# A four-stage hybrid trunk on one core: gate and up weights handed over separately, the down product's PSUM banks one by one, and an 80-row meta matrix

## What is computed

```python
for i in range(DEPTH):                      # DEPTH = 2
    mix = pool_mixer(...) if i == 0 else latent_attention_mixer(...)
    x = layer_norm(ALPHA * x + mix, ...)
    x = layer_norm(ALPHA * x + swiglu(x, w_gate[i], w_up[i], w_down[i]), ...)

def swiglu(h, w_gate, w_up, w_down):        # 1024 x 2816, 1024 x 2816, 2816 x 1024
    return (silu(h @ w_gate) * (h @ w_up)) @ w_down
```

## Time and profile before

| | us |
|---|---|
| median of 3 runs | 2686.84 |
| lowest and highest | 2685.57 and 2687.7 |
| the profiled execution's own time | 2684.7 |
| its span, first to last instruction | 2682.9 |

### The profile page before, as it was taken

How to read it: one execution, slowest core, us unless ns; L and a number is a source line. 1 busy time by engine, 2 the same in 40 slices (tenths; PEclk the granted TensorE clock), 3 DMA queues, 4 the chain that set the end, 5 groups by cost and what they waited for, 6 DMA issues and landing times.

```text
span 2682.9 us, 34788 instructions
## 1 busy us (share of the span) xinstructions
PE 2553.1 (95%) x13203; PEld 2122.1 (79%) x13203; DVE 1005.3 (37%) x1489; ACT 567.6 (21%) x948; POOL 585.6 (22%) x290
## 2 busy tenths in 40 slices
PE   8899999999999889899999999988999999999996
PEld 7789888898889776585857584447889988899885
DVE  3433333333333642333333333422333333333336
ACT  2411011110111342332323232433111111111112
POOL 2422222222222410000000000232222222222225
PEclk9999999999999989999999999988999999999998
DMA  5201110111101111000000002232101111011111
GB/s 165 55 24 47 47 47 23 47 47 47 47 23 47 44 48 43 16 1 31 0 19 12 16 0 75 80 122 55 46 25 47 47 47 40 30 47 47 47 31 67
DMA packets 130114, 117.37 MB, mean 44 GB/s; under 512 B 8704, under 2 KB 117208, under 8 KB 130048
## 3 DMA queue, kind: packets, MB, share of 16 engines
q1 hardware_dynamic: 130064, 116.70, 14.6%
HBM read 110.81 MB, written 6.42 MB: 44 GB/s over the span
## 4 chain that ended last, share of the span: by engine, by line
PE 92%; DVE 4%; issue 2%; ACT 1%; POOL 0%; DMA 0%; SPq 0%; ACTq 0%; DVEq 0%
PE ps L557 22%; PE ps L558 21%; PE ps L559 21%; PE ps L922 4%; PE ps L911 4%; PE ps L806 2%; PE ps L895 2%; PE ps L978 1%; PE ps L780 1%; PE ps L822 1%; PE ps L811 1%; PE ps L627 1%; PE ps L953 1%; PE ps L851 1%; PE ps L937 1%
## 5 line engine op out<-in xcount | busy, mean ns | idle before, releaser
L557 PE MATMUL ps<-XH,WGH 128*128 128x368 f32 x2112 | 699.8, 331 | 17.6 <-POOL WGL L1700 13.5
L558 PE MATMUL ps<-XL,WGH 128*128 128x368 f32 x2112 | 700.0, 331 | 0.0
L559 PE MATMUL ps<-XH,WGL 128*128 128x368 f32 x2112 | 697.2, 330 | 0.0
L1452 DVE TENSOR_TENSOR XR<-XR,ps 128x1024 f32<-128x1024 f32 x378 | 461.5, 1221 | 105.7 <-PE ps L559 105.7
L557 PEld LDWEIGHTS ps<-XH,WGH 128*128 128x128 f32 x2112 | 398.5, 189 | 22.3 <-issue 18.9
L1437 DVE TENSOR_TENSOR HF<-SG,ps 128x368 f32<-128x368 f32 x132 | 71.0, 538 | 917.8 <-PE ps L559 912.6
L558 PEld LDWEIGHTS ps<-XL,WGH 128*128 128x128 f32 x2112 | 398.0, 188 | 1.8
L559 PEld LDWEIGHTS ps<-XH,WGL 128*128 128x128 f32 x2112 | 398.2, 189 | 0.0
L557 PE MATMUL ps<-WDH,HH 128*128 128x512 f32 (+1 forms) x792 | 329.4, 416 | 9.6 <-DVE XR L1452 9.6
L1691 POOL TENSOR_TENSOR HL<-HF,HH 128x368 fp32r<-128x368 f32 x132 | 129.8, 983 | 853.0 <-DVE HH L1441 853.0
L559 PE MATMUL ps<-WDH,HL 128*128 128x512 f32 (+1 forms) x792 | 314.9, 398 | 0.0
(11 more groups left out here) (205 smaller groups left out, 2725.8 us busy)
## 6 DMA issues: line engine op xcount, KB each, us to landing
RAWG<-ffn_w_gate SPq DMA_DIRECT2D x44, 512.0 KB, 4.7
RAWG<-ffn_w_up SPq DMA_DIRECT2D x44, 512.0 KB, 5.9
RAWD<-ffn_w_down SPq DMA_DIRECT2D x44, 512.0 KB, 3.7
CR<-cache_mla_l SPq DMA_DIRECT2D x64, 160.0 KB, 2.6
XR<-x_prompt SPq DMA_DIRECT2D x8, 512.0 KB, 12.4
WOP<-mla_w_o SPq DMA_DIRECT2D x4, 1024.0 KB, 5.0
WOA<-mla_w_o SPq DMA_DIRECT2D x1, 4096.0 KB, 17.3
o_y_prompt<-XR SPq DMA_DIRECT2D x8, 512.0 KB, 2.6
```

The lines of the kernel that those rows point to most:

```text
L557: pe.matmul(out, w[0], x[0], start=start, stop=False)
L558: pe.matmul(out, w[0], x[1], start=False, stop=False)
L559: return pe.matmul(out, w[1], x[0], start=False, stop=stop)
L1452: dve.tensor_tensor(XR[0:r, t, :], XR[0:r, t, :], bank2(4 + 2 * w, r), ALU.add).then_inc(s_row[2 * l + 1], 1)
```

## The change

- **Gate and up weights.** Loads, splits and handovers are made for each of the two apart. SP counts them in `f_raw[l][0]` and `f_raw[l][1]`; ACT copies 1024 elements twice, the gate half as soon as the last gate product of the block before is done (`f_gmm`), the up half after the last up product (`f_umm`). POOL subtracts twice. TensorE waits for the gate half ahead of the first gate product, and for the up half ahead of the first up product. ACT's copy of the gate half stands ahead of the third silu of a block, and POOL's two subtractions stand ahead of its third `HL`. SP loads block 1 of gate and up ahead of the next layer norm's gain and bias, and down of block 1 behind them.
- **Down product.** Waits and counts go by single banks: three matmuls, one addition of 512 columns, four banks in turn (`BANKS = 4`). The last down products and the layer norm's waits follow.
- **Meta matrix.** `BM` is loaded with 80 rows, of which rows 16 to 79 are zero, and the product takes all 80 rows of tile 8. The result is the same.

```diff
-            sp.dma_start(BM[0:META], a["c_band_meta"]).then_inc(s_band, 16)
+            sp.dma_start(BM[0:TAIL], a["c_band_meta"]).then_inc(s_band, 16)
...
-                        ins = pe.matmul(o, XR[0:META, 8, ch], BM[0:META, g, :], start=False, stop=True)
+                        ins = pe.matmul(o, XR[0:TAIL, 8, ch], BM[0:TAIL, g, :], start=False, stop=True)
...
                 for m, done in ((0, f_gmm[l]), (1, f_umm[l])):
+                    if j == 0:
+                        pe.wait_ge(f_glo[l], 2 * n + m + 1)
                     for c in range(DC):
...
             def gate_up(l, n, even):
-                pe.wait_ge(f_glo[l], n + 1)
...
-                pe.wait_ge(s_row[2 * l + 1], NT * n + t + 1)
                 for half in (0, 1):
                     ds = slice(half * 512, half * 512 + 512)
-                    ins = split_product(ps[0:r, 4 + 2 * w + half, :], (HH[:, b, cols(t)], HL[:, b, cols(t)]),
-                                        (WDH[:, ds], WDL[:, ds]), True, True)
-                ins.then_inc(f_dmm[l], 1)
+                    pe.wait_ge(s_row[2 * l + 1], 2 * NT * n + 2 * t + half + 1)
+                    split_product(ps[0:r, 4 + 2 * w + half, :], (HH[:, b, cols(t)], HL[:, b, cols(t)]),
+                                  (WDH[:, ds], WDL[:, ds]), True, True).then_inc(f_dmm[l], 1)
...
-            def split_gate_up(l, n):
-                act.wait_ge(f_raw[l], 32 * (n + 1))
-                act.wait_ge(f_umm[l], 3 * n)
-                act.wait_ge(f_glo[l], n)
-                copy(WGH[:], RAWG[:]).then_inc(f_ghi[l], 1)
+            def split_gate_up(l, n, m):
+                act.wait_ge(f_raw[l][m], 16 * (n + 1))
+                if not (isinstance(n, int) and n == 0):
+                    act.wait_ge((f_gmm, f_umm)[m][l], 3 * n)
+                    act.wait_ge(f_glo[l], 2 * n - 1 + m)
+                copy(WGH[:, m], RAWG[:, m]).then_inc(f_ghi[l], 1)
...
-                dve.tensor_tensor(XR[0:r, t, :], XR[0:r, t, :], bank2(4 + 2 * w, r), ALU.add
-                                  ).then_inc(s_row[2 * l + 1], 1)
+                for half in (0, 1):
+                    ds = slice(half * 512, half * 512 + 512)
+                    dve.wait_ge(f_dmm[l], 1 + 2 * NT * n + 2 * t + half + 1)
+                    dve.wait_ge(s_row[2 * l + 1], 2 * NT * n + 2 * t + half + 1)
+                    dve.tensor_tensor(XR[0:r, t, ds], XR[0:r, t, ds], ps[0:r, 4 + 2 * w + half, :], ALU.add
+                                      ).then_inc(s_row[2 * l + 1], 1)
```

## The result

| | median (us) | range | runs |
|---|---|---|---|
| before | 2686.20 | 2684.24 to 2687.70 | 4 |
| after | 2621.54 | 2615.64 to 2626.25 | 4 |

The ratio is 0.9759, with a 95% interval from 0.9732 to 0.9785. The profiled execution after took 2625.73 us, with a span of 2623.9. Against the span of before, 2682.9, the two traces differ by 59.0 us.

The account below looks back on a forecast made before the run. TensorE was taken to bound the kernel, holding 92% of the chain. Gains of 26 + 17.5 + 7 = 50.5 us gave 2684.7 - 50.5 + 2.1 = 2636.3 us, 1.9% less, with a range of 2631 to 2650.

Parts of the forecast that it names:

- the 50.5 us of the sum: Whole kernel: total gain expected, 26 for the down product, 17.5 for gate and up, 7 for the opening.
- the down product's term: The 40 down products in the loops: single banks remove a loss of 0.65 us each, 26 us in all.
- the tails, put at 0: Ends of both FFNs: dearer split additions and an earlier first piece put at 0, 1 us to either side.
- gate and up: Block 1 of each FFN: halves remove stops of 6.72 and 6.75 us and the low clock behind them, 17.5 us.
- the opening: Tile 0's window sums: 80 rows give 0.213 us a matmul instead of 0.361, gaining 7 us, bounds 0 and 7.5.
- the 2.1 us added to get to the median: Whole kernel: the median of before lay 2.1 us above its profiled execution, so 2.1 was added to the forecast.
- DVE's pace: Down product: additions of 512 columns follow each other at 0.69 to 0.72 us, so DVE keeps up with TensorE.
- The yardstick: Down product: undisturbed matmuls take 0.233 us each, so 54 would take 12.58 us instead of 13.23.
- the whole loss: Down product: all 0.65 us lost in each of 40 products is regained, 26 us, also the term's upper bound.
- The margins: Block 1 of gate and up: both halves arrive 0.1 to 0.2 us before TensorE wants them.
- the 0.4 us of waits: Block 1 of gate and up: an allowance of 0.1 us of wait for each of four halves.
- the third part: Opening: 80 rows in the meta matrix, 7 us; a rival that they don't help had a chance of 0.12.

Follow-up runs that it names:

- e2: Kernel before with only the down product's banks handed over one by one: 2649.47 us, ratio 0.9866.
- e3: Kernel before with only gate and up weights loaded, split and handed over separately: 2663.97 us, ratio 0.9926.
- e4: Kernel before with only the meta matrix taken to 80 rows: 2677.18 us, ratio 0.9974.
- e12: The changed kernel run again without an edit: 2619.68 us (2618.02 to 2624.48, 5 runs).
- e6: The changed kernel without an edit, for one more profile: one run, 2618.54 us.
- e8: The changed kernel with 64 rows in the meta matrix instead of 80: one run, 2634.81 us.

## Why the prediction was right and wrong

**The places and mechanisms of the three parts were right.** They act where the rows put them, each alone as much as together (e2 to e4). The time still missed the range. Against the 50.5 us of the sum stand 59.0 between the profiles and 62.5 to 65.0 between the medians of three sets of runs. Of the 14.8 us by which the forecast was too high, 8.5 are in the sum: the down product's term was 4.1 too small, the tails, put at 0, gave 4.8, gate and up 0.8 more, and the opening 1.1 less. The other 6.3 us are the step from the profiled execution to the median. The steps that failed are three: the size of the down product's term, the tails put at 0, and the 2.1 us added to get to the median.

**Down product: 26 predicted, 30.1 measured.** DVE's pace was right, 0.68 us an addition where the text has 0.69 to 0.72. The yardstick failed. I took the undisturbed 0.233 us of `last_down` for the loop, whose matmuls run at 0.231. Over 54 matmuls and 40 products, 0.002 us each are 4.3 us. The change didn't make the matmuls of `last_down` faster: 42 of them take 9.79 us after as well, 0.233 each. In `last_down` the products of two blocks alternate in a bank. Whether that is the reason I didn't test. In the loop before, the matmuls between two waits stood 0.232 apart on average. Worse, I gave "the whole loss" as the upper bound of that term, so the range had no room above it.

**Gate and up: 17.5 predicted, 18.3 measured.** No stop and no low clock. Everything there lies 5.9 us earlier, by the opening. With these added, ACT starts the halves at 114.46 and 118.49, where the text has 114.45 and 118.48, and POOL ends at 118.02 and 122.05 (text: 118.0 and 122.1). The margins, 0.1 to 0.2 us in the text, were 0.22 for the up half, and both held; the 0.4 us of waits that I allowed weren't needed and are half of the 0.8 that the term was short.

**Opening: 7 predicted, 5.9 in the profile, 8.6 in e4.** 80 rows run at 0.21 us a matmul, as forecast. Three steps of the sum were off. The first matmul isn't fixed at 7.85: it starts between 8.30 and 10.24 in all other profiles, and those with 16 rows (7.85 to 9.01) overlap with those with 80 (8.32 to 10.24). The clock doesn't rise by the same delay each time: it rose 6.5 us after the first matmul in the profile after, 4.0 in e4 and e12, and 3.5 in e6, where I had 6. Together they make the 2.7 us between the profile after and e4. And `L627` didn't wait for DVE: in e4 it starts at 17.42, right behind the last window sum, with DVE's copy done at 17.12. So that the 7 lies between the two measured values is in part luck.

The text weighed a rule from "TensorE: Matmul & The Clock Gate" in the Trainium skill, that the number of rows in a weight load doesn't matter, and took it to mean that the third part would give nothing. For the load itself the traces agree with it: between 10 and 14 us a load takes 308 ns on average with 16 rows (before) and 310 with 64 (e8), 310 with the 128 beside them, and 333 with 80 (after). Most of the time lies between the loads. With 16 or 64 rows in turn with 128, no weights are loaded for 0.22 us ahead of each change of the number of rows, which is 0.22 of the 0.30 us that a product takes longer; with 80 rows the loads have no such gap. What the engine does in these 0.22 us the traces don't show.

**Tails: 0 predicted, 4.8 in the profile, 2.5 in e12.** The text had 1 us either way. It counted the lengths of the additions and left out which engine would start first on the next pair of instructions. At tiles 2 and 3, pairs of banks put POOL ahead by 0.13 us; the earlier first half takes that lead away. In the first tail it is a matter of 0.01 us then, and luck for a single execution. In the second tail DVE, if it comes second there, comes first at tiles 5 and 6. Why the one goes with the other wasn't followed up.

**Profile against median.** I added 2.1 us to go from the profiled execution to the median. The executions of before lie within 3 to 4 us of each other in four sets of runs (within 10 in the fifth); those of the changed kernel spread over 6.5 to 10.6 us in three, and its profiled one is among the longest. The 3.5 to 6 us that the medians gain beyond the 59.0 I put down to executions with less time at the low clock in the attention part, as in e6 and e12; a profile of each execution would be needed to show it. Before has only one profile, so why its executions seldom get there is open.

## What to carry to other kernels

Take the pace of undisturbed matmuls from the loop itself where a wait is to be costed: 0.002 us in each of 54 matmuls is a seventh of the loss. Where two buffers are handed over as a pair, look first at whether the consumer could free them one by one; it was the largest part here, and it cost DVE nothing on the path. And where DVE and POOL both work on SBUF in a chain, look at which starts first: a tie decides as much as a stage of the work.

## What the runs showed of the hardware

**Rows of the weights.** In the opening, matmuls whose weights have 128 rows in turn with 16 or 64 are 0.36 us apart on average, and in turn with 80 they are 0.21, like 128 alone. The load of 16 or 64 rows is no longer than that of 128; at each change between them TensorE loads nothing for 0.22 us. I hadn't expected 64 to be as slow as 16. All this is from the opening, at the low clock.

**DVE and POOL in SBUF.** An addition of two SBUF operands takes DVE 1.23 us where it starts first and up to 3.47 behind POOL's gain; the gain takes POOL 2.39 where it starts first and up to 3.46 behind DVE. Additions with a PSUM operand keep their 0.69 us beside POOL's work. A POOL instruction of 0.20 us made the tail 1.9 us shorter.

**The clock of a part that wasn't touched.** The same kernel ran its attention part in 763.6 or 770.8 us, with 59.9 or 73.7 us of it at the low clock. A gain under 7 us on a kernel like this needs the stretches, not one profile.
